# Eight modulation tiles and a gate row move to the end of a recurrent block

## The reference, cut to what matters

```python
# odd mixed layer, end
return x + jnp.concatenate([y_c, y_d, y_m], axis=-1) @ w_out        # K = 1280, N = 1024
# second block, layer 0
mod = (jax.nn.silu(c) @ ada_w[l] + ada_b[l])[:, None, :]            # 1024 x 6144
sh1, sc1, g1, sh2, sc2, g2 = jnp.split(mod, 6, axis=-1)
h = rmsnorm(x, norm_mix_g[l]) * (1.0 + sc1) + sh1
y = rglru_block(h, ...)
x = x + g1 * y
h = rmsnorm(x, norm_ffn_g[l]) * (1.0 + sc2) + sh2
x = x + g2 * peer(h, ...)
# rglru_block
gate_in, rec_in = jnp.split(h @ w_in, 2, axis=-1)
gate = jax.nn.gelu(gate_in, approximate=False)
xc = conv_b + sum(xp[:, k:k + S] * conv_w[k] for k in range(4))
r, i = sigmoid(blocks(xc) @ wa + ba), sigmoid(blocks(xc) @ wx + bx)
log_a = -8 * r * softplus(-lam); a = exp(log_a)
b = sqrt(-expm1(2 * log_a)) * (i * xc)
hs = scan(a, b)                                                      # along the sequence
return (gate * hs) @ w_out
```

## Time and profile before

| | us |
|---|---|
| timed runs | 2472.56, 2474.60, 2509.92 |
| median of them | 2474.6 |
| profiled execution, device time | 2471.42 |
| its span, first to last instruction | 2470.2 |
| mean granted TensorE clock | 0.985 |

### The profile page before, as it was taken

One profiled execution on the slowest core, in us unless ns is written; L12 is line 12 of the kernel. 1 busy time (PEld: TensorE's weight loads), 2 busy tenths in 40 slices (PEclk: granted clock), 3 DMA queues, 4 the chain that ended last, 5 costly groups with the idle time before them and its releaser, 6 DMA issues. The chain is left out here.

```text
span 2470.2 us, 37755 instructions
## 1 busy us (share of the span) xinstructions
PE 2341.4 (95%) x11671; PEld 1913.4 (77%) x11671; DVE 1917.5 (78%) x4361; ACT 1157.1 (47%) x2034; POOL 153.6 (6%) x172
## 2 busy tenths in 40 slices
PE   7998998899898999999999989898899999999997
PEld 5775466667787888888888856687788888888886
DVE  5677778757997788888888856599877777777776
ACT  5674247242285444444444435415844444444443
POOL 0000000000351000000000000014400000000000
PEclk9999999999999999999999999999999999999999
DMA  6524640653213667666777641222155555555553
GB/s 257 183 104 141 238 159 22 228 199 115 77 35 122 227 251 261 254 254 247 258 254 255 253 167 69 88 84 69 38 194 192 194 190 187 188 192 193 190 187 136
DMA packets 144615, 429.31 MB, mean 174 GB/s; under 512 B 15231, under 2 KB 21375, under 8 KB 144511
## 3 DMA queue, kind: packets, MB, share of 16 engines
q1 hardware_dynamic: 144510, 428.08, 48.8%
HBM read 426.99 MB, written 1.05 MB: 173 GB/s over the span
## 5 line engine op out<-in xcount | busy, mean ns | idle before, releaser
L3396 PE MATMUL bank<-v_parts,weighted_high 128*128 128x512 f32 x1952 | 531.2, 394 | 6.0 <-DVE weighted_low L3536 6.0
L3382 PE MATMUL bank<-h_t_parts,u_t_high 128*128 128x512 f32 x1824 | 450.5, 389 | 0.0
L3396 PEld LDWEIGHTS bank<-v_parts,weighted_high 128*128 128x128 f32 x1952 | 352.8, 190 | 70.8 <-issue 7.5
L3382 PEld LDWEIGHTS bank<-h_t_parts,u_t_high 128*128 128x128 f32 x1824 | 342.3, 188 | 71.1
L3476 ACT ACTIVATE activated<-activated 128x256 f32<-128x256 f32 x228 | 95.6, 419 | 476.5 <-DVE activated L3524 476.5
L3457 ACT ACTIVATE u_t_high<-u_ring 128x1024 fp32r<-128x1024 f32 x228 | 241.3, 1058 | 163.3 <-DMA u_ring<-in_peer_u 161.9
L3396 PE MATMUL bank<-v_parts,weighted_low 128*128 128x512 f32 x976 | 302.8, 391 | 0.0
L3511 DVE TENSOR_TENSOR u_t_low<-u_ring,u_t_high 128x1024 fp32r<-128x1024 f32 x228 | 278.7, 1222 | 30.1 <-ACT u_t_high L3457 26.8
L3518 DVE TENSOR_TENSOR v_parts<-v_ring,v_parts 128x1024 fp32r<-128x1024 f32 x242 | 294.4, 1217 | 3.3 <-ACT v_parts L3464 3.3
L3464 ACT ACTIVATE v_parts<-v_ring 128x1024 fp32r<-128x1024 f32 x242 | 255.1, 1054 | 71.1 <-PE bank L3396 70.9
L3385 PEld LDWEIGHTS bank<-h_t_parts,u_t_low 128*128 128x128 f32 x1824 | 248.8, 190 | 17.8
(11 more groups left out here) (593 smaller groups left out, 3543.7 us busy)
## 6 DMA issues: line engine op xcount, KB each, us to landing
v_ring<-in_peer_v SPq DMA_DIRECT2D x244, 512.0 KB, 3.3
u_ring<-in_peer_u SPq DMA_DIRECT2D x228, 512.0 KB, 4.5
panel<-in_l_w_in SPq DMA_DIRECT2D x15, 2048.0 KB, 8.1
late_tiles<-in_ada_w SPq DMA_DIRECT2D x54, 512.0 KB, 4.3
mod_ring<-in_ada_w SPq DMA_DIRECT2D x42, 512.0 KB, 4.7
panel<-in_peer_w_q SPq DMA_DIRECT2D x8, 2048.0 KB, 7.7
panel<-in_l_w_out SPq DMA_DIRECT2D x4, 2560.0 KB, 8.8
early_u<-in_peer_u SPq DMA_DIRECT2D x20, 512.0 KB, 3.4
```

The source lines that it names most:

```text
L3382: nc.tensor.matmul(banks[2 + k][:, :], UTH[:, k, j, :], H2[:, j, :, :].rearrange("p a s -> p (a s)"), start=(j == 0), stop=False, skip_gro ...
L3396: last = nc.tensor.matmul(banks[4 + 2 * t + half][:, :], w[:, t * P:(t + 1) * P], v[k][:, half * 512:(half + 1) * 512], start=opens and n ...
```

## The change

Three things are moved.

The second mixed layer's output projection has no modulation steps any more. All later tiles move down by eight: the recurrent block's existing adds now take tiles 18 to 33, and a new `modulation.add(f, dve, 16)` behind the last scan takes tiles 34 to 41. On SyncE the loads for it stand behind the first query panel (`outs[1] + 1`).

The diagonal of g1, which needs tiles 16 to 23, goes from before the softplus to before `mults(0)`; the two products from behind ("rec", 0) to behind ("gel", 2); the two copies from behind `conv(0)` to behind `states(1)`.

```diff
@@ -2522,7 +2522,7 @@
                      LRU_ROWS_AT, gains=gain_work([(0, sc1, C("norm_mix_g_2", 0, 8))], 0, 16),
                      ready={4: (rows_d, 1), 6: (rows_c, NT)},
                      at_act={0: act_squares, 1: lambda act: sqrt_table(), 2: act_root, 3: act_silu},
-                     at_dve={0: dve_gated, 1: dve_mean, 2: dve_scale, 4: dve_conv}, mod_steps=(0, 16), plain=2)
+                     at_dve={0: dve_gated, 1: dve_mean, 2: dve_scale, 4: dve_conv}, mod_steps=(0, 0), plain=2)
 
     lru_rows = odd_output()
 
@@ -2619,6 +2619,8 @@
                 modulation.load(sp, 6)
                 load_panels(sp, outs[1])
                 modulation.load(sp, 6)
+                load_panels(sp, outs[1] + 1)
+                modulation.load(sp, 16)
                 load_panels(sp, outs[1] + 3)
 
             @block.tensor
@@ -2654,7 +2656,7 @@
                                 last = nc.tensor.matmul(acc_bank(g)[:, h * S:(h + 1) * S], w[:, 2 * n + k, h * P:(h + 1) * P],
                                                         XC[:, 2 * n + k, :], start=(k == 0), stop=(k == 1))
                         last.then_inc(acc_ready, 1)
-                    if job == ("rec", 0):
+                    if job == ("gel", 2):
                         pe.wait_ge(diag_ready, 1)
                         for i in range(2):
                             nc.tensor.matmul(banks[4 + i][:, :], ONES[:, :],
@@ -2798,15 +2800,9 @@
                 f(v.tensor_tensor(SPL[:, 2, :], SPL[:, 1, :], lamc, ALU.min), exp_in)
                 f(v.memset(RC[:, :, 0:LP], 0.0), wait=False)
                 f(v.memset(ONES[:, :], 1.0), wait=False)
-                f(v.tensor_tensor(MOD[:, 16:24], MOD[:, 16:24], C("ada_b_2", 16, 8), ALU.add))
-                f(v.tensor_tensor(DIAG[:, :, :], ident[:, :].unsqueeze(1).broadcast_to([P, KD, P]),
-                                  g1.unsqueeze(2).broadcast_to([P, KD, P]), ALU.mult), diag_ready)
                 softplus()
                 modulation.add(f, dve, 4)
                 conv(0)
-                for i in range(2):
-                    dve.wait_ge(row_ready, i + 1)
-                    f(v.tensor_copy(GROW[:, i * 512:(i + 1) * 512], banks[4 + i][:, :]), row_stored, wait=False)
                 modulation.add(f, dve, 4)
                 conv(1)
                 modulation.add(f, dve, 4)
@@ -2816,6 +2812,9 @@
                 modulation.add(f, dve, 4)
                 decays(0)
                 modulation.add(f, dve, 2)
+                f(v.tensor_tensor(MOD[:, 16:24], MOD[:, 16:24], C("ada_b_2", 16, 8), ALU.add))
+                f(v.tensor_tensor(DIAG[:, :, :], ident[:, :].unsqueeze(1).broadcast_to([P, KD, P]),
+                                  g1.unsqueeze(2).broadcast_to([P, KD, P]), ALU.mult), diag_ready)
                 mults(0)
                 modulation.add(f, dve, 4)
                 states(0)
@@ -2824,6 +2823,10 @@
                 mults(1)
                 modulation.add(f, dve, 4)
                 states(1)
+                for i in range(2):
+                    dve.wait_ge(row_ready, i + 1)
+                    f(v.tensor_copy(GROW[:, i * 512:(i + 1) * 512], banks[4 + i][:, :]), row_stored, wait=False)
+                modulation.add(f, dve, 16)
                 gain_work([(1, sc2, C("norm_ffn_g_2", 0, 8))], 24, 40)(f)
                 dve.wait_ge(row_stored, 2)
                 for i in range(2):
```

## The result

| | before | after |
|---|---|---|
| median of the timed runs, us | 2475.97 (20 runs) | 2466.90 (20 runs) |
| lowest run | 2471.09 | 2461.20 |
| ratio, with its 95% interval | | 0.9943 [0.9917, 0.9969] |
| profiled execution, its time | 2471.42 | 2470.28 |
| its span | 2470.2 | 2469.1 |

A forecast was written before the change was run, and what follows sets the result against it. The projection half was taken as bound by VectorE and its tiles, the recurrent block mostly by TensorE; -6.8 + 0.4 = -6.4 us from 2472.9 gave 2466.5, rounded to 2467, range 2462 to 2474.

The forecast's parts named there:

- the term for the rest of the program: Everything behind the recurrent block is released by events and only shifts with it; no further gain or loss.
- The level: Starting time of the kernel before, 2472.9 us, the mean of three executions that agree.
- Part one: Second mixed layer's output projection, second half: without its eight tiles TensorE runs unbroken, saving 6.8 us.
- Rows 5: Profile rows of the first mixed layer's same projection half, 13.77 us unbroken, taken as the time to expect.
- Part two: Gate row leaves the recurrent block's front: row products cost 1.7 us, earlier gelu panel gains 1.3; sum +0.4 us.
- Part three: Recurrent block: diagonal and copies at their new places hold no products, the diagonal covered by more than 10 us.
- Part four: Eight adds at the recurrent block's end cost 0, with 4.6 us to spare before the last evacuation.
- the larger gain: Rival: gelu panel takes 9.0 us or less, block changes by -1.5; total -8.3, 2464.6 us; chance 0.13.
- The half clock after the longer wait: Rival: slow stretch after TensorE's 2.0 us gelu panel wait loses 1.5 us; total -4.9, 2468.0 us; chance 0.10.
- Late tail: Rival: tiles behind the query panel each take 9.1 us, costing +4.0; total -2.4, 2470.5 us; chance 0.08.
- slower: Rival: five last tiles come one at a time, costing +10.9; total +4.5, 2477.4 us; chance 0.04.
- no effect: Rival: something else holds the projection half, or the expert stage gives the time back; 2472.9 us; chance 0.05.

The follow-up runs named there:

- dummy_adds: Changed kernel plus eight dummy VectorE reductions, without loads, at the old places in the projection's second half; mean 2475.1 us.
- row_wait: Changed kernel with the gate row's diagonal behind conv(1) and its adds, its two products behind ("rec", 3); ratio 0.9943, mean 2468.1 us.
- panel_first: Changed kernel with the first gelu panel issued ahead of the loads of the block's third and fourth tiles; mean 2466.7 us, ratio 0.9964.
- gate_late: Kernel before with only the gate row moved, the eight tiles staying in the projection; ratio 0.9997, mean 2474.3 us.
- tail_plus_six: Changed kernel plus six dummy reductions behind the eight adds at the block's end; block 113.13 us.
- before_a: Kernel before run again without an edit, for a second profile; projection plus block 155.98 us.
- after_third: Changed kernel run a third time without an edit; mean 2468.1 us, ratio 0.9975.
- before_b: Kernel before run again without an edit, for a third profile; projection plus block 155.72 us.
- four_and_four: Kernel variant keeping four of the eight tiles in the projection's second half and moving four to the block's end; mean 2467.6 us.
- no_tail: Changed kernel with the last eight early tiles neither loaded nor reduced, their columns set to zero; mean 2468.9 us.
- delay_late: Changed kernel plus nine dummy products in the latent output projection, behind the latent attention; mean 2476.3 us.

## Why the prediction was right or wrong

**The time** was forecast at 2467 and measured at 2466.9, but this is luck: two errors cancel, a level 3.0 us too low and a change 2.4 us too small. The forecast change is -6.4 us. Measured are -8.8 between the means, -9.1 between the medians and -14 by the ratio, of which some 4.5 us are before's long executions that only this ratio keeps. The sum of the prediction, -6.4 for the two stages that it worked out, is what those two stages show: -6.4.

**The step that failed is the term for the rest of the program, put at nothing:** "Everything behind the block is released by events and shifts with it." It does shift, and no code of it was changed, yet the means show another 2.4 us (standard error 0.7) outside the two stages. The same sentence leaves no room for what the stages behind the block do by themselves from one execution to the next, which is more than the change is worth (8.6 and 29.8 us in the attention alone). The third timed run, 2509.92, was set aside as lying apart, with no term for how often such a run comes in either sample. Why the means differ by the 2.4 us stays open.

**The level failed beside it.** "I take 2472.9, the mean of the three that agree" was a level from three executions; the mean over 125 is 2475.9. The profiled execution of before was among the fastest 15 of these, and not for the two stages, which took 155.3 us in it and 155.75 on the mean of four.

**Part one, -6.8:** right. -6.82 between the two profiled executions, -6.5 on the means of four and three. Rows 5 were the right neighbour: 13.77 us there, 13.76 here. The split, which I had left as one sum, is in part shown: 3.2 for the pace by dummy_adds, 3.3 for the late tile by subtraction.

**Part two, +0.4:** +0.70 between the two profiled executions, +0.1 on the means. The gelu panel was to be issued 1.3 us sooner, counted from the block's start: on the means of four and three profiles it is (24.27 and 22.99 us), between the two first profiles only 0.46, because the block's first products of after ran at the lower clock for longer. The products on it start 1.6 us sooner on the means, not 1.3, as the panel also took 10.7 us instead of 11.0; 1.7 - 1.6 is the measured +0.1. The wait in after was 1.38 us, not 2.0: its panel took 10.5 us. The slow first products do not explain it, for they delay the panel's issue and the end of the rec products alike, by 0.8 us. That the row products fill no wait at their new place was right, and row_wait and panel_first show what this costs: 1.6 to 1.8 us.

**Part three:** the diagonal was hidden, the copies too; gate_late shows no cost.

**Part four, 0:** right. The adds ended at 543.2, the first evacuation was some 1.6 us late (1.2 forecast), the spare time measured 4.2 us (4.6 forecast). One wait of 2.7 us was named; there were three, of 3.43, 1.26 and 0.75. The sum came out near all the same: counted from the block's start the adds ended at 95.4 us, 94.8 forecast.

**The rivals:** the larger gain needed the panel to land sooner on its own; it did not, and took a change of SyncE's order. The whole change, -8.8 us, lies near this rival's -8.3, but not by its mechanism. The estimate of 7 us that the prediction sets beside this rival is from a section on transfers that GpSimd issues, and SyncE issues all panels here; the first gelu panel took 10.5 to 11.3 us in the profiles of both kernels. The half clock after the longer wait did not come at 1.4 to 1.7 us (1.00 from 481 to 489 in after), and came at 2.7 us in dummy_adds. Late tail, slower, and no effect: not seen.

## What to carry to other kernels

Small work that is placed beside an engine-bound stage has two prices, its pace on that engine and the place of its loads in the queue; here they were about equal, and half of the work was free in the old place. Work that must be done anyway belongs where its engine waits for another's long run, if its loads are not put behind a large one. And a saving of a quarter of a percent can be read from the changed stages of one profile of each (6.1 us here, 6.4 on several), but neither the level nor the difference between whole executions can: those need tens of executions of each, with the long ones treated alike on both sides. Where a single stage time also holds a clock that differs, the gap at the end of the stage, in the same trace, is the better measure, as in tail_plus_six.

## What the runs showed of the hardware

The granted clock of a stage differs between executions of the same program. The latent attention took 39.12 us at clock 1.00 in before's first profile, 47.69 us at 0.79 in before_a, and 68.92 us at 0.50 in after_third. The rows are from the window view, columns as in the earlier trace rows; 1.00 stands for the level of 2.4 GHz and 0.50 for that of 1.2:

```profile
1510.08:1549.20 39.12, 37.45 (x257) 32.51 (x257) 32.41 (x128) 31.29 (x97) 0.00 (x0) 1.00 0.03 12
```

```profile
1513.14:1560.83 47.69, 46.73 (x257) 40.17 (x257) 32.61 (x128) 31.46 (x97) 0.00 (x0) 0.79 0.00 1
```

```profile
1506.97:1575.89 68.92, 68.21 (x256) 58.98 (x257) 32.53 (x128) 31.81 (x97) 0.00 (x0) 0.50 0.00 1
```

The products are the same, TensorE is busy for 46.73 or 68.21 instead of 37.45 us, and VectorE's work is nearly unchanged. Twelve of the twenty profiles show the first length, three the second and five the third (before_b, after_third, four_and_four, no_tail, delay_late), and these five are the profiled executions of 2495 us and more. Their 30 us are thus mostly one stage at the lower level (68.92 - 39.12 = 29.8). What decides the level that the stage gets is not shown. Time and mean clock go together from execution to execution: even under 2495 us, the changed kernel's first 20 runs range from 2461.2 us at 0.987 to 2474.05 at 0.979, which is more than the change itself is worth.

The Trainium skill, "TensorE: Matmul & The Clock Gate", Part 1, says that the point where the clock turns varies from run to run. The rows agree that it differs, and show 8.6 and 29.8 us for one stage deep inside the program.
